# A hybrid decoder trunk: residual sums turned unscaled, by halves; norm weights applied at the eviction into high and low parts, reciprocal roots applied to the outputs of the projections

## The chip, the cores and the metric

The kernel runs on one core of a Trainium2 chip. The metric is the device time in microseconds of one execution. Its engines are named as the profile names them: PE (TensorE), DVE (VectorE), ACT (ScalarE), POOL (GpSimd) and SP (SyncE, which here only issues DMAs).

## The reference, cut to what matters

Two layers over 256 tokens of width 1024. The change is about how the norm in front of a projection is computed; the mixers in between keep their arithmetic.

```python
def rms_norm(x, g):
    y = x * lax.rsqrt(jnp.mean(x * x, axis=-1, keepdims=True) + NORM_EPS)
    return y * g

for l in range(DEPTH):                       # DEPTH = 2
    h = rms_norm(h_res, norm_mix[l])         # "norm 0" (l = 0), "norm 2" (l = 1)
    u = h @ w_in[l]                          # 1024 x 2536
    y = ...                                  # four mixers (MLA, NSA, RG-LRU, SSD) on columns of u
    h_res = h_res + y @ w_out[l]
    h = rms_norm(h_res, norm_ffn[l])         # "norm 1" (l = 0), the expert norm (l = 1)
    if l % 2 == 0:
        f = swiglu(h, ffn_w_gate[l // 2], ffn_w_up[l // 2], ffn_w_down[l // 2])
    else:
        f = moe_ffn(h, ...)                  # top 2 of 8 experts
    h_res = h_res + f
return rms_norm(h_res, norm_final)
```

The root of a row (a token) and the weight of a column commute with the product: `(x * r[t] * g[c]) @ W = r[t] * ((x * g[c]) @ W)`. The change uses this.

## The kernel before, in words

Tokens lie on the 128 partitions in two blocks (`tb` 0 and 1; `TB` = 2), each with 1024 columns in `xres`. All weights pass in pieces of 1 MB through a ring of seven slots (`ring`), loaded by SP in the order of use; a slot is loaded again once the DVE has read it (`lo_ready`). Products are made in three parts of reduced-precision float: ACT copies a piece into its high part (`w_hi`, `split`, L1228 and L1250), DVE subtracts to get the low part (`w_lo`, L1636 and L1661), and PE adds up high by high, high by low and low by high (`products3`, L413 to L415). One piece is 24 matmuls of 512 columns. Piece `p` of the mixer and its successors are called by their number here; `p + 1` is the second half of the inner dimension of the first columns.

Every engine runs its own written-out program in order and waits on semaphores. So what sets the order around the change is the place of a call in each engine's program.

**A norm before the change** (`turn_normed`, L386, on PE; `normed`, L1599, on DVE; `split_input`, L1230 and on, on ACT):

1. DVE adds the projection's sums to `xres` (`add_sums`, L1639 and on; L1643). The last piece is ordered so that block 0 is complete first and signals `proj_done`; block 1 is complete with the piece (`units_used`).
2. ACT squares and sums a block (`mean_square`, L1215); POOL turns the mean into the reciprocal root `rstd` (`roots`, L1122 and L1123).
3. DVE scales the block into `hn` (L1603; for norm 0 ACT does it, L1293).
4. PE turns `hn`, 16 transposes of 128 x 128 (L393), into four banks of PSUM.
5. DVE multiplies each bank by the norm weight into `hT` (L1612), ACT copies it into `hT_hi` (L1234), DVE subtracts into `hT_lo` (L1617). PE waits on `hT_lo_ready` for each half of the inner dimension before its products.

Banks 0 to 3 are those that DVE empties (`bank(0)`, `dve_took`), banks 4 to 7 those that ACT empties (`bank(1)`, `act_took`). The mixer's first projection (`by_token`) writes banks 4 to 7. The dense FFN (`ffn`) writes banks 0 to 3 first, and PE therefore waits in front of it until every bank that was given to DVE has been taken:

```python
                pe.wait_ge(act_took, gave[1])
                pe.wait_ge(dve_took, gave[0])
                if l == 0:
                    ffn(TB, BASE_FFN[0], hT_hi, hT_lo, BASE_FFN[0], 0)
```

At the start, SP loads `x`, then twelve small sets of parameter rows (`rows`, L1024, and `pe_row`, L1038), and only then the weights. PE turns the parameter rows into `par` (L404, L406; DVE L1589, L1590), which holds the norm weights among others.

In the mixer, ACT evicts the first projections into `utok` (L1314) and four banks into `xraw` (L1337); DVE evicts four banks into `lraw` (L1769), two into `xraw` (L1823) and two into `zs` (L1826). The convolutions read `lraw` and `xraw` (`conv`, L1798 and L1801). `cin` (L1832) needs ACT's `kvcT` (L1352).

In front of the experts the sums are already turned unscaled (L849), multiplied with the router (L862), and the root is applied to the logits.

## Time and profile before

| | us |
|---|---|
| median of 3 runs | 1603.23 (1601.26 to 1603.72) |
| the profiled execution, its own time | 1601.23 |
| its span in the trace | 1599.7 |
| DVE busy | 1249.2 (78%) |
| ACT busy | 1001.2 (63%) |
| POOL busy | 73.2 (5%) |
| mean granted TensorE clock | 0.971 of full speed |

A span begins with the first instruction and ends with the last; the execution's own time is 1.5 us longer. "Idle before" is the time that an engine stood still in front of an instruction, and behind the arrow stands the instruction that ended it.

### The profile page before, as it was taken

What the parts mean: (1) busy time and instruction counts of PE and PEld (TensorE: products, weight loads), DVE (VectorE), ACT (ScalarE), POOL (GpSimd) and SP (SyncE); (2) the same over time, 40 slices, a digit from 0 to 9 for tenths busy, and PEclk for the clock granted to TensorE, in tenths of its full rate; (3) what the DMA queues carried; (4) which work ended last, traced back from release to release, by engine and by line L of the source; (5) the groups of instructions that cost most, each with busy time, mean ns of one, the idle gap of its engine ahead of it and who ended that gap; (6) DMA issues with size and microseconds to landing.
All of it is one profiled execution on the core that took longest, in us unless ns stands there. A gap on an engine that the chain in (4) does not pass through costs nothing.

```text
span 1599.7 us, 20439 instructions
## 1 busy us (share of the span) xinstructions
PE 1538.3 (96%) x7566; PEld 1289.0 (81%) x7566; DVE 1249.2 (78%) x1286; ACT 1001.2 (63%) x911; POOL 73.2 (5%) x105
## 2 busy tenths in 40 slices
PE   7989899999899899999999999999999999999996
PEld 5978688888688787887888888888888888888884
DVE  6776744444458787999988988988988988989985
ACT  6456443344353556777777777778778777777763
POOL 2101000000000001000000000000000000000000
PEclk9987999999999799999999999999999999999998
DMA  9700655555452035999999999999999999999990
GB/s 294 242 1 15 187 190 194 191 184 183 131 168 70 1 101 186 393 397 348 393 396 347 394 397 346 394 397 345 394 398 344 395 397 344 396 396 345 395 389 29
DMA packets 189741, 444.25 MB, mean 278 GB/s; under 512 B 9617, under 2 KB 15902, under 8 KB 189678
## 3 DMA queue, kind: packets, MB, share of 16 engines
q1 hardware_dynamic: 185214, 427.82, 72.8%
q0 software_dynamic: 4464, 15.58, 3.8%
q8 instruction: 40, 0.66, 0.2%
q14 instruction: 23, 0.19, 0.0%
HBM read 435.51 MB, written 7.86 MB: 277 GB/s over the span
## 4 chain that ended last, share of the span: by engine, by line
PE 92%; DVE 5%; ACT 1%; issue 1%; SPq 0%; POOL 0%; DMA 0%; POOLq 0%; ACTq 0%; DVEq 0%
PE bank L414 26%; PE bank L415 26%; PE bank L413 26%; PE bank L543 2%; PE bank L470 2%; PE bank L546 1%; PE bank L682 1%; PE bank L664 1%; PE bank L641 1%; DVE work L1801 1%; PE bank L692 1%; PE bank L656 1%; DVE hT L1612 0%; PE bank L700 0%; DVE work L1854 0%
## 5 line engine op out<-in xcount | busy, mean ns | idle before, releaser
L1661 DVE TENSOR_TENSOR w_lo<-ring,w_hi 128x2048 fp32r<-128x2048 f32 x372 | 846.3, 2290 | 182.1 <-ACT w_hi L1250 180.9
L1250 ACT ACTIVATE w_hi<-ring 128x2048 fp32r<-128x2048 f32 x372 | 711.8, 1916 | 230.1 <-PE bank L413 230.1
L414 PE MATMUL bank<-w_hi,xT_hi 128*128 128x512 f32 x896 | 353.5, 394 | 0.5 <-DVE xT_lo L2225 0.5
L415 PE MATMUL bank<-w_hi,xT_lo 128*128 128x512 f32 x896 | 349.5, 390 | 0.0
L413 PE MATMUL bank<-w_lo,xT_hi 128*128 128x512 f32 x896 | 239.9, 389 | 0.0
L414 PE MATMUL bank<-w_hi,hidT_hi 128*128 128x512 f32 x560 | 220.8, 394 | 2.7 <-DVE hidT_lo L1668 2.7
L415 PE MATMUL bank<-w_hi,hidT_lo 128*128 128x512 f32 x560 | 218.4, 390 | 0.0
L413 PEld LDWEIGHTS bank<-w_lo,xT_hi 128*128 128x128 f32 x896 | 168.2, 188 | 35.5
L414 PEld LDWEIGHTS bank<-w_hi,xT_hi 128*128 128x128 f32 x896 | 168.2, 188 | 34.5 <-DVE xT_lo L2225 0.7
L415 PEld LDWEIGHTS bank<-w_hi,xT_lo 128*128 128x128 f32 x896 | 168.4, 188 | 33.8
L414 PE MATMUL bank<-w_hi,hT_hi 128*128 128x512 f32 (+2 forms) x384 | 149.5, 393 | 9.9 <-DVE hT_lo L1617 9.9
L415 PE MATMUL bank<-w_hi,hT_lo 128*128 128x512 f32 (+2 forms) x384 | 147.9, 388 | 0.0
L413 PE MATMUL bank<-w_lo,hidT_hi 128*128 128x512 f32 x560 | 147.8, 389 | 0.0
L414 PEld LDWEIGHTS bank<-w_hi,hidT_hi 128*128 128x128 f32 x560 | 105.2, 188 | 24.6 <-DVE hidT_lo L1668 3.4
L413 PEld LDWEIGHTS bank<-w_lo,hidT_hi 128*128 128x128 f32 x560 | 105.1, 188 | 22.3
L415 PEld LDWEIGHTS bank<-w_hi,hidT_lo 128*128 128x128 f32 x560 | 105.2, 188 | 21.3
L1256 ACT ACTIVATE hidT_hi<-bank 128x512 fp32r<-128x512 f32 x70 | 41.2, 599 | 101.4 <-PE bank L470 101.4
L1636 DVE TENSOR_TENSOR w_lo<-ring,w_hi 128x2048 fp32r<-128x2048 f32 (+1 forms) x34 | 77.1, 2280 | 30.2 <-ACT w_hi L1228 30.0
L414 PEld LDWEIGHTS bank<-w_hi,hT_hi 128*128 128x128 f32 x384 | 74.4, 194 | 24.8 <-issue 7.4
L413 PE MATMUL bank<-w_lo,hT_hi 128*128 128x512 f32 (+2 forms) x384 | 91.6, 380 | 0.0
L1228 ACT ACTIVATE w_hi<-ring 128x2048 fp32r<-128x2048 f32 (+1 forms) x34 | 64.4, 1900 | 39.7 <-PE bank L413 24.5
L415 PEld LDWEIGHTS bank<-w_hi,hT_lo 128*128 128x128 f32 x384 | 74.4, 194 | 13.9
(355 smaller groups left out, 1372.1 us busy)
## 6 DMA issues: line engine op xcount, KB each, us to landing
ring<-in_moe_w_gate_dram SPq DMA_DIRECT2D x112, 1024.0 KB, 9.5
ring<-in_moe_w_up_dram SPq DMA_DIRECT2D x112, 1024.0 KB, 9.4
ring<-in_moe_w_down_dram SPq DMA_DIRECT2D x112, 1024.0 KB, 9.1
ring<-in_ffn_w_gate_dram SPq DMA_DIRECT2D x14, 1024.0 KB, 5.1
ring<-in_ffn_w_up_dram SPq DMA_DIRECT2D x14, 1024.0 KB, 5.2
ring<-in_ffn_w_down_dram SPq DMA_DIRECT2D x14, 1024.0 KB, 4.9
ring<-in_w_in_dram SPq DMA_DIRECT2D x12, 1024.0 KB, 5.2
ring<-in_w_out_dram SPq DMA_DIRECT2D x8, 1024.0 KB, 8.4
```

The costliest lines, as they stand in the source:

```text
L413: return pe.matmul(o, x_hi, w, start=False, stop=stop)
L414: pe.matmul(o, x_hi, w, start=start, stop=False)
L415: return pe.matmul(o, x_lo, w, start=False, stop=False)
L470: mm = pe.transpose(banks[2 + v][:, f * P:(f + 1) * P], hid[:, v, f * P:(f + 1) * P], ident[:, :])
L543: mm = pe.matmul(b[i][:, 0:S], wk, hT_hi[:, 4 * h + k, :], start=start and not low, stop=stop and low)
L546: pe.matmul(b[i][:, 0:S], wk, hT_lo[:, 4 * h + k, :], start=False, stop=False)
L641: mm = pe.matmul(b[:, i * nk:(i + 1) * nk], q, k, start=True, stop=True)
L1228: act.activation(dst[:, :, 0:n], slot_k(p)[:, :, 0:n], ACT.Copy).then_inc(hi_ready, 1)
L1250: act.activation(w_hi[:, (base + at) % SPLIT, :], ring[:, i, :], ACT.Copy).then_inc(hi_ready, 1)
L1256: act.activation(hidT_hi[:, v, :], banks[2 + v][:, :], ACT.Copy).then_inc(hidT_hi_ready, 1)
L1636: dve.tensor_tensor(dst[:, :, 0:n], slot_k(p)[:, :, 0:n], hi[:, :, 0:n], ALU.subtract)\
L1661: dve.tensor_tensor(w_lo[:, v, :], ring[:, (base + at) % RING, :], w_hi[:, v, :].bitcast(F32), ALU.subtract).then_inc(lo_ready, 1)
```

## The change

Norms 0, 1 and 2 lose the scaling pass. PE turns `xres` itself, each half of a block as soon as its sum is added (`turn_sums`); ACT evicts each bank straight into `hT_hi` with the norm weight as scale, and DVE makes `hT_lo` from the same bank in one instruction (two instructions of 256 columns for a bank on either engine). The root now goes elsewhere: into the scale of the `utok` evictions, into SiLU's scale and the product behind it in the dense FFN, and, where the outputs have channels on the partitions, as a row `rrow` that PE spreads over the partitions from two diagonal matrices (`rdiag`). The last piece of each output projection is ordered by halves of a block, and `add_sums` waits for each half. DVE splits the first piece of the second mixer ahead of the sums. At the start, the parameter rows are issued from ACT's queue instead of SP's, `ident` is made first, and PE turns six blocks of `x` before the parameter rows.

```diff
+            def turn_half(norm, b, tb, g):
+                for k in range(2):
+                    mm = pe.transpose(b[:, (2 * k + tb) * P:(2 * k + tb + 1) * P],
+                                      xres[:, tb, (2 * g + k) * P:(2 * g + k + 1) * P], ident[:, :])
+                if tb == TB - 1:
+                    give(mm, 0)
+
+            def turn_sums(norm):
+                mark["raw", norm] = gave[0]
                 b = [bank(0) for _ in range(4)]
                 for tb in range(TB):
-                    pe.wait_ge(hn_ready, TB * norm + tb + 1)
...
+                    for h in range(2):
+                        pe.wait_ge(half_added, 4 * (norm - 1) + 2 * tb + h + 1)
+                        for g in (2 * h, 2 * h + 1):
+                            turn_half(norm, b[g], tb, g)
+            pe.wait_ge(ident_ready, 1)
+            pe.wait_ge(x_in, 16 * TB)
...
-                        if first:
-                            pe.wait_ge(hT_lo_ready, 8 * l + 2 * h + 2)
...
+                                    if first and tb == 0 and k % 2 == 0 and not low:
+                                        pe.wait_ge(dve_took, mark["raw", 2 * l] + 2 * h + k // 2 + 1)
...
+                pe.wait_ge(rdiag_ready, l + 1)
+                b = bank(1)
+                for tb in range(TB):
+                    mm = pe.matmul(b[:, tb * P:(tb + 1) * P], ones[:, :], rdiag[:, tb, :], start=True, stop=True)
+                give(mm, 1)
...
-            sp.wait_ge(prow_zero, 1)
-            rows("mix", norm_mix.rearrange("l (a b) -> a l b", b=P), 8)
...
+            act.wait_ge(prow_zero, 1)
+            rows("mix", norm_mix.rearrange("l (a b) -> a l b", b=P), 8)
...
-            def split_input(norm):
+            def split_turned(norm):
                 for g in range(4):
-                    act.wait_ge(dve_took, mark["turned", norm, g])
-                    act.activation(hT_hi[:, 2 * g:2 * g + 2, :], hT[:, 2 * g:2 * g + 2, :], ACT.Copy)\
-                        .then_inc(hT_hi_ready, 1)
+                    n = mark["raw", norm] + g
+                    act.wait_ge(*filled_by[0][n])
+                    for k in range(2):
+                        hi = act.activation(hT_hi[:, 2 * g + k, :], banks[n % 4][:, k * S:(k + 1) * S], ACT.Copy,
+                                            scale=par[:, l, c0 + 2 * g + k:c0 + 2 * g + k + 1])
+                    hi.then_inc(hT_hi_ready, 1)
...
+                b = filled()
+                act.activation(rrow[:, :], b[:, 0:S], ACT.Copy).then_inc(act_took, 1)
...
-            def normed(l2, turn_set):
-
-                for tb in range(TB if l2 else 0):
-                    dve.wait_ge(rstd_ready, 7 * (l2 // 2) + 5 * (l2 % 2) + tb + 1)
-                    signal(dve.tensor_scalar(hn[:, tb, :], xres[:, tb, :],
...
+            def split_turned(norm):
+                for g in range(4):
+                    b = filled()
+                    dve.wait_ge(hT_hi_ready, 4 * norm + g + 1)
+                    for k in range(2):
+                        at = 2 * g + k
+                        lo = dve.scalar_tensor_tensor(out=hT_lo[:, at, :], in0=b[:, k * S:(k + 1) * S],
+                                                      scalar=par[:, l, c0 + at:c0 + at + 1],
+                                                      in1=hT_hi[:, at, :].bitcast(F32), op0=ALU.mult, op1=ALU.subtract)
+                    take_bank(lo)
...
+            def add_sums(stage, unit):
+                for tb in range(TB):
+                    for half in range(2):
+                        if (tb, half) == (TB - 1, 1):
+                            dve.wait_ge(units_used, unit + 1)
+                        else:
+                            dve.wait_ge(proj_done, 3 * stage + 2 * tb + half + 1)
+                        r = xres[:, tb, half * 512:(half + 1) * 512]
+                        signal(dve.tensor_tensor(r, r, banks[4 + 2 * tb + half][:, :], ALU.add), "half", half_added)
...
-                    take_bank(dve.tensor_copy(lraw[:, i, 3:3 + S], b[:, 0:S]))
+                    take_bank(dve.tensor_tensor(lraw[:, i, 3:3 + S], b[:, 0:S], rrow[:, :], ALU.mult))
...
+                link(dve.tensor_tensor(xraw[:, 0:4, 3:3 + S], xraw[:, 0:4, 3:3 + S],
+                                       rrow.unsqueeze(1).broadcast_to([P, 4, S]), ALU.mult))
```

How the order of the instructions moves, at three places. A row is one instruction or several alike (`x8`), with its line, operation, what it writes and reads, and the size.

ACT, from the start of its program to the third piece of weights, before:

```order
L1215 ACT_TABLE_LOAD
L1215 ACTIVATE hn,stat<-xres 128x1024 x2
L1293 ACTIVATE hn<-xres,rstd 128x1024 x2
L1228 ACTIVATE w_hi<-ring 128x2048
L1234 ACTIVATE hT_hi<-hT 128x512 x4
L1228 ACTIVATE w_hi<-ring 128x2048
L1228 ACTIVATE w_hi<-ring 128x4x496
```

And now, from the last three of the twelve DMAs on:

```order
L1224 DMA prow<-in_mla_kv_norm_dram 1x256
L1224 DMA prow<-in_mla_q_norm_dram 2x2x96
L1238 DMA pe_row<-in_nsa_cmp_pe_dram 32x4x64
L1218 ACT_TABLE_LOAD
L1218 ACTIVATE hn,stat<-xres 128x1024 x2
L1250 ACTIVATE w_hi<-ring 128x2048
L1260 ACTIVATE hT_hi<-bank,par 128x256 x8
L1250 ACTIVATE w_hi<-ring 128x2048
L1250 ACTIVATE w_hi<-ring 128x4x496
```

The scaling L1293 is gone, the twelve DMA issues stand in front of the table load, and the first piece still stands ahead of the eviction into `hT_hi`.

ACT at norm 2 (between the dense FFN and the second mixer), before:

```order
L1256 ACTIVATE hidT_hi<-bank 128x512 x2
L1250 ACTIVATE w_hi<-ring 128x2048
L1228 ACTIVATE w_hi<-ring 128x2048
L1215 ACTIVATE hn,stat<-xres 128x1024 x2
L1228 ACTIVATE w_hi<-ring 128x2048
L1234 ACTIVATE hT_hi<-hT 128x512 x4
L1228 ACTIVATE w_hi<-ring 128x4x496 x2
```

And now:

```order
L1283 ACTIVATE hidT_hi<-bank 128x512 x2
L1277 ACTIVATE w_hi<-ring 128x2048
L1250 ACTIVATE w_hi<-ring 128x2048 x2
L1260 ACTIVATE hT_hi<-bank,par 128x256 x8
L1218 ACTIVATE hn,stat<-xres 128x1024 x2
L1250 ACTIVATE w_hi<-ring 128x4x496 x2
```

The squares moved from ahead of the turned sums to behind them, and both pieces of the first projection stand ahead.

DVE at the same place, before:

```order
L1643 TENSOR_TENSOR xres<-xres,bank 128x512 x4
L1705 MEMSET work 128x2x3
L1706 MEMSET work 128x6x3
L1636 TENSOR_TENSOR w_lo<-ring,w_hi 128x2048
L1710 MEMSET router 128x56
L1713 TENSOR_TENSOR router<-router,par 128x64
L1603 TENSOR_SCALAR hn<-xres,rstd 128x1024 x2
L1612 TENSOR_TENSOR hT<-bank,par 128x512 x3
L1617 TENSOR_TENSOR hT_lo<-hT,hT_hi 128x512
L1612 TENSOR_TENSOR hT<-bank,par 128x512
L1617 TENSOR_TENSOR hT_lo<-hT,hT_hi 128x512 x3
```

And now:

```order
L1677 TENSOR_TENSOR xres<-xres,bank 128x512 x2
L1678 COPY flag<-ones 128x1
L1677 TENSOR_TENSOR xres<-xres,bank 128x512 x2
L1678 COPY flag<-ones 128x1
L1644 SCALAR_TENSOR_TENSOR hT_lo<-bank,par,hT_hi 128x256 x8
L1665 TENSOR_TENSOR w_lo<-ring,w_hi 128x2048
L1743 MEMSET work 128x2x3
L1744 MEMSET work 128x6x3
L1665 TENSOR_TENSOR w_lo<-ring,w_hi 128x4x496
L1751 TENSOR_SCALAR hn<-ident,rstd 128x128 x2
```

Eight instructions of 256 columns stand where ten of 512 or 1024 did, and the split of a piece and the router's rows no longer lie between the sums and the norm.

## Rows read from the trace of the kernel before

**Rows 1.** The page: busy us of the engines, and the chain that ended last by engine.

```profile
PE 1538.3 (96%) x7566; PEld 1289.0 (81%) x7566; DVE 1249.2 (78%) x1286; ACT 1001.2 (63%) x911; POOL 73.2 (5%) x105
...
PE 92%; DVE 5%; ACT 1%; issue 1%; SPq 0%; POOL 0%; DMA 0%; POOLq 0%; ACTq 0%; DVEq 0%
```

**Rows 2.** Timeline of the start: start us, us, engine, line, operation, idle before.

```profile
1.70 0.37 SPq L1024 DMA_DIRECT2D prow<-in_norm_mix_dram  x1
...
5.30 0.32 SPq L1038 DMA_DIRECT2D pe_row<-in_nsa_cmp_pe_dram  x1
5.66 19.48 SPq L982 DMA_DIRECT2D ring<-in_w_in_dram  x10
...
8.09 0.66 PE L404 MATMUL bank<-ident,prow 128*128 128x128 f32 x2 [8.09 <-DMA pe_row<-in_nsa_cmp_pe_dram]
...
10.84 1.91 ACT L1228 ACTIVATE w_hi<-ring 128x2048 fp32r<-128x2048 f32 x1 [0.34 <-DMA ring<-in_w_in_dram]
...
16.63 0.79 PE L414 MATMUL bank<-w_hi,hT_hi 128*128 128x512 f32 x1 [3.08 <-DVE hT_lo L1617]
...
21.35 0.40 PE L415 MATMUL bank<-w_hi,hT_lo 128*128 128x512 f32 x1
...
26.54 2.23 DVE L1636 TENSOR_TENSOR w_lo<-ring,w_hi 128x1984 fp32r<-128x1984 f32 x1
...
29.74 3.65 ACT L1228 ACTIVATE w_hi<-ring 128x1984 fp32r<-128x1984 f32 x2
```

**Rows 3.** Timeline of PE and DVE at norm 1, before the dense FFN.

```profile
181.42 1.07 PE L413 MATMUL bank<-w_lo,hT_hi 128*128 128x512 f32 x4
...
182.60 1.41 DVE L1643 TENSOR_TENSOR xres<-xres,bank 128x512 f32<-128x512 f32 x2 [1.38 <-PE bank L413]
...
192.32 0.77 PE L414 MATMUL bank<-w_hi,hT_hi 128*128 128x512 f32 x1 [3.52 <-DVE hT_lo L1617]
...
196.29 0.39 PE L415 MATMUL bank<-w_hi,hT_lo 128*128 128x512 f32 x1
```

**Rows 4.** Timeline of PE and DVE at norm 2, before the second mixer.

```profile
429.48 1.07 PE L413 MATMUL bank<-w_lo,hidT_hi 128*128 128x512 f32 x4
...
432.38 2.29 DVE L1636 TENSOR_TENSOR w_lo<-ring,w_hi 128x2048 fp32r<-128x2048 f32 x1
...
442.86 0.76 PE L414 MATMUL bank<-w_hi,hT_hi 128*128 128x512 f32 x1 [3.28 <-DVE hT_lo L1617]
...
448.22 0.39 PE L415 MATMUL bank<-w_hi,hT_lo 128*128 128x512 f32 x1
```

**Rows 5.** Windows: engines' busy us (instructions), PEclk, DMA share, GB/s.

```profile
183.00:186.00 3.00, 1.06 (x6) 1.09 (x7) 1.72 (x3) 1.96 (x3) 1.02 (x3) 0.84 0.00 0
...
434.00:438.00 4.00, 2.07 (x10) 2.10 (x11) 2.47 (x5) 1.05 (x1) 1.74 (x2) 0.52 0.51 146
```

**Rows 6.** Durations of like instructions, from the timeline.

```profile
74.27 0.39 ACT L1344 ACTIVATE work<-bank 128x256 f32<-128x256 f32 x1 [0.37 <-PE bank L578]
74.55 0.38 ACT L1345 ACTIVATE work<-bank 128x256 f32<-128x256 f32 x1
74.64 1.53 DVE L1801 SCALAR_TENSOR_TENSOR work<-work,par 128x256 f32<-128x256 f32 x3
...
98.52 0.42 DVE L1877 TENSOR_TENSOR work<-bank,work 128x256 f32<-128x256 f32 x1
...
416.77 1.03 PE L470 MATMUL bank<-ident,work 128*128 128x128 f32 x8
```

**Rows 7.** Timeline of DVE in the mixers: the last evictions, and `cin` behind them.

```profile
78.64 0.90 DVE L1823 COPY work<-bank 128x256 f32<-128x256 f32 x2 [0.19 <-PE bank L543]
...
82.43 1.16 DVE L1832 TENSOR_TENSOR work<-work,pe_t 128x240 f32<-128x240 f32 x2 [1.93 <-ACT work L1355]
...
508.85 1.17 DVE L1832 TENSOR_TENSOR work<-work,pe_t 128x240 f32<-128x240 f32 x2 [1.93 <-ACT work L1355]
```

**Rows 8.** Timeline in front of the experts.

```profile
606.10 1.41 DVE L1643 TENSOR_TENSOR xres<-xres,bank 128x512 f32<-128x512 f32 x2 [1.57 <-PE bank L413]
```

More of the change, by code:

```diff
@@ L439, in project @@
                                 t = slice(i * P, (i + 1) * P)
+                                if n == TB and bank0 == 0 and c == 0 and i == 0 and k % 2 == 0 and not low:
+                                    pe.wait_ge(dve_took, mark["raw", 1] + 2 * h + k // 2 + 1)
                                 mm = products3(banks[bank0 + (c * n + i) % 2][:, :], x_hi[:, 4 * h + k, t],
@@ L460, in down @@
                                                c == 0 and h == 0 and f == 0, last and f == 1, low)
-                        if last and low and i < n - 1:
+                        if n == TB and last and low and (i, halves) != (n - 1, (1,)):
                             mm.then_inc(proj_done, 1)
@@ L810, in project_output @@
                     last = i == 3
-                    order = [(tb, low) for tb in range(TB) for low in (False, True)] if last else \
-                        [(tb, low) for low in (False, True) for tb in range(TB)]
-                    for tb, low in order:
+                    order = [(tb, low, (half,)) for tb in range(TB) for half in range(2) for low in (False, True)] \
+                        if last else [(tb, low, (0, 1)) for low in (False, True) for tb in range(TB)]
+                    for tb, low, halves in order:
                         w = parts_of(p, p, i, low).rearrange("p (k n) -> p k n", k=2)
-                        for half in range(2):
+                        for half in halves:
                             for k in range(2):
@@ L820, in project_output @@
                                                last and k == 1, low)
-                        if last and low and tb == 0:
+                        if last and low and (tb, halves) != (TB - 1, (1,)):
                             mm.then_inc(proj_done, 1)
```

215 lines of the change are left out of this document (106 added, 109 removed).

## The prediction, before the changed kernel ran

> **What bounds the kernel.** I read the page first: PE is busy for 96% of the span, and the chain that ended last lies on PE for 92% of it and on DVE for 5% [rows 1]. So PE's work is what the span consists of, and a change that leaves PE's matmuls as they are can gain only where PE stands still or runs slowly. I then read the timeline of PE and found three such places that belong to a norm. At each, PE ends one projection, waits for adding, squaring, root, scaling, turning, weighting and splitting, and starts the next: at the start (first product at 16.63) [rows 2]; at norm 1, from 182.49 (181.42 + 1.07) to 192.32, 9.8 us [rows 3]; at norm 2, from 430.55 to 442.86, 12.3 us [rows 4]. The windows add that the granted clock falls while PE idles (0.84 in 183 to 186, 0.52 in 434 to 438, so it is at the lower of its two levels, 1.2 GHz instead of 2.4) [rows 5]. The timeline of PE shows what this costs behind each gap: products at 2.4 GHz start 0.23 us apart (four in 1.07, the last of them 0.39 [rows 3]), at 1.2 GHz 0.43 us. Behind the start there are 11 intervals in 4.72 us (16.63 to 21.35), which would take 2.5 at the higher level: 2.2 us lost. Behind norm 1, 11 intervals in 3.97 (192.32 to 196.29): 1.4 lost. Behind norm 2, 13 intervals in 5.36 (442.86 to 448.22): 2.4 lost [rows 2 to 4].
>
> **Norm 2, step by step.** Call the end of the last matmul E (430.55). The new adds of the first three quarters lie inside the last piece: a half takes 6 of its 24 matmuls, 1.36 us, and an add 0.70 (1.41 for two, [rows 3]). The last one starts with the same delay as now (0.11 us, 182.49 to 182.60) and ends at E + 0.8. The 16 transposes cost 0.13 each at full clock [rows 6]; 12 of them wait for nothing and take until E + 1.5, the last four end near E + 2.0, but the first bank is complete after ten, at E + 1.3. ACT then evicts a bank with two instructions of 0.38 that start 0.28 apart [rows 6]: 0.66 for the first bank, E + 2.0. DVE follows with two of 256 columns. The nearest row is the same operation at this size in SBUF, 1.53 for three, so 1.0 for a bank with its wait [rows 6]: E + 3.0. The first product needs only this bank, and the next bank comes 1.0 us later, as long as four products take. So PE starts at E + 3.0 instead of E + 12.3: 9.3 saved. The split of the first piece, 2.29 on DVE between the adds and the norm [rows 4], costs nothing now, since it stands ahead of the adds where DVE waits. PE idles only from E + 2.0 to E + 3.0, less than in any of the gaps above behind which it was slow, so I give back the 2.4 of the slow products too. Sum for norm 2: -11.7. Squares and roots stay on ACT and POOL behind the evictions (E + 3.8 to about E + 7), hidden by the first two pieces, 10.9 us of PE, before anything reads a root.
>
> **Norm 1** has the same chain, but one more wait: the dense FFN writes banks 0 to 3, and PE first waits until DVE has taken all four. DVE gives the last one free at E + 3.0 + 3 x 1.0 = E + 6.0, and if its pairs overlap (0.85) at E + 5.5; I take 5.7. Saved: 9.8 - 5.7 = 4.1. PE idles for 3.7 us in front of it. The clock was still high in most of 183 to 186 [rows 5], and fell in an idle stretch of like length, so the loss lies between 0 and 2.4; I take 1.2, against 1.4 now. Sum: -4.3.
>
> **The start.** SP now issues the first weights where the first parameter row stood, at 1.70 instead of 5.66, and the first piece lands 5.2 us or less after its issue (5.66 to 10.84) [rows 2]. It has `x` (1 MB) in front of it, so it lands between 6.9 and 10.8; I take 8.7. The parameter rows take ACT twelve issues of 0.3 (1.2 to 4.9) as they took SP, and the table load moves behind them, which costs ACT's squares 0.4 us. They landed by 8.09 after the last issue at 5.30 [rows 2]; now I expect some 8.3. PE has turned six blocks of `x` by then, turns the parameters (1 us), and the other ten blocks by 11.7. ACT splits the first piece until 10.6 (1.91), evicts the first bank until 11.3, DVE its low part until 12.3. First product at 12.3 instead of 16.63: -4.3, with 11.5 and 16.6 as its bounds. The slow products behind it stay: in 1.9 of loss (the mean of the three) for 2.2: -0.3. Sum: -4.6. DVE's chain of small work (angles, lambda) ended at 26.54, and ACT's small work behind it at 29.74 [rows 2], where it takes the fourth piece. Now DVE does four banks (to 15.3), two splits (4.6) and 4.6 us of small work: 24.5. ACT takes the fourth piece at 27.7 and has it at 29.6, and PE wants it at 12.3 + 10.9 + 1.9 + 5.3 = 30.4. That is the thinnest cover of the change; gone, it would cost what is missing at this one place.
>
> **In front of the experts** the adds of block 1 run one after the other behind the piece (606.10 + 1.41) [rows 8]. Now one lies inside the piece, and the router's products start 0.7 earlier: -0.6.
>
> **What is added.** PE: two matmuls of 128 columns for each layer. No row shows them; transposes of that size cost 0.13 [rows 6], and products with a plain operand may cost two to three times that. Bounds 0.3 and 0.9 a layer, I take 0.4: +0.8. ACT: one eviction of 0.4 for each layer behind the last `utok`, beside PE's channel projections: 0. DVE: `lraw`, `xraw` and `zs` are multiplied where they were copied. A product from PSUM of 256 columns takes 0.42 [rows 6], a copy 0.45 [rows 7]: 0. The scaling of four `xraw` channels, 1024 columns, is new; 512 columns cost 0.70 and 2048 cost 2.29, so about 1.2. It delays the evictions behind it, but DVE then stands idle 1.93 us for ACT in both layers [rows 7]: 0, and if that cover were gone 1.2 a layer. The 14 products with SiLU's output in the FFN get a scalar and keep their size, beside PE: 0.
>
> For the eviction in two pieces the rows say 0.66 on ACT and 1.0 on DVE for a bank, as against 0.70 for one instruction of 512. The Trainium skill speaks against such pieces (VectorE: DVE Perf Modes, "The TRN2 errata"): many small tiles pay the fixed latency each time, and it advises at least 512 elements. By its formula for two-source fp32, (N + 151) / 0.96, a pair would cost 0.85 us, and norm 1 would gain 0.4 us more than by the rows; the formula is for a plain two-tensor operation, and no run here shows it for this one.
>
> **Sum.** -11.7 - 4.3 - 4.6 - 0.6 + 0.8 = -20.4. Against the profiled execution's own 1601.2 this is 1580.8; the median of the runs is 2.0 above that execution, so I forecast 1582.5 for a median.
>
> **Rivals.**
> 1. *The parameter rows come late.* Now megabytes of weights are in flight beside them, while before they were ahead of every weight. If they land 4 us later, the first product stays at 16.6, and the result is 1587. For it: the queue is full from the start. Against it: they are small. The Trainium skill says (DMA: Bandwidth & Descriptors, "Issuing engines are not separate DMA queues") that transfers issued by different engines run on the same 16 engines and interleave; by that they would be slowed and not held up.
> 2. *The same on the other side.* If they are served only behind the ring's pieces, whose ten issues end at 25.14 (5.66 + 19.48) and the last of which lands 5.2 later, they land at about 33 (25.1 + 5.2 + 2.7, as now from issue to use), and the first product comes 3.5 later, at 36.5: 19.9 late. The other terms give 15.8 back: +4.1, 1607. From a first product at 32.4 on (16.6 + 15.8) the kernel is slower than before. No row shows a transfer held up like this.
> 3. *The mixers take it back.* DVE's chain there is tight: it came to the last evictions 0.19 us before PE had filled the bank [rows 7]. If products from PSUM cost 0.3 more than copies (8 of them) and the 1.2 of the scaling is not hidden, this is +3.6 a layer: 1590.
> 4. *The clock stays low.* If PE falls to 1.2 GHz at norm 1 and norm 2 as before, 2.4 and 1.2 come back: 1586.
>
> **Chances.** The forecast (1577 to 1585) 0.6; rival 1 0.12, rival 3 0.12, rival 4 0.1; rival 2 and anything else that ends above 1606.4, 0.03; within 0.2% (3.2 us, about what a measurement of this kernel can tell from no change) 0.03. Faster is all the rest, 0.94. The range must take in rivals 1, 3 and 4, and below the forecast a start at 11.5, banks freed at E + 5.3 and no slow products at norm 1: 1575 to 1590.
>
> **What would show it.** The first product near 12.3; the gap at norm 2 of about 3 us with products 0.23 apart behind it, and of 5.7 at norm 1; `cin` with 0.7 us of idle time left in front of it; the parameter rows' transposes before 9. A first product after 16, a gap at norm 2 above 5, or a second layer's mixer that is longer than before would make it wrong.

## The result, and the profile after

The changed kernel took 1587.28 us (median of 4 runs, 1584.44 to 1589.42) beside 1603.34 for the kernel before: a ratio of 0.9903, 95% interval 0.9888 to 0.9919. The forecast was 1582.5 with a range from 1575 to 1590: faster, as forecast, but by 16.1 us, not by 20.8. Twelve more runs in two later groups had medians of 1589.09 and 1589.57, so the median of all 16 is 1589.1 and the shortfall rather 6.6 than 4.8.

| | before | after |
|---|---|---|
| profiled execution, own time / span (us) | 1601.23 / 1599.7 | 1585.41 / 1583.6 |
| mean granted clock | 0.971 | 0.974 |
| first product | 16.63 | 15.97 |
| gap at norm 1 | 9.83 | 5.80 |
| gap at norm 2 | 12.31 | 3.12 |

The page of after, against [rows 1]: busy us of PE, and the chain by engine. PE has 8 more matmul records and 1.7 us less busy time; the share of the span is 97%.

```profile
PE 1536.6 (97%) x7574; PEld 1290.4 (81%) x7574; DVE 1246.5 (79%) x1292; ACT 1002.8 (63%) x923; POOL 74.3 (5%) x105
...
PE 93%; DVE 4%; ACT 1%; issue 1%; DMA 0%; ACTq 0%; POOL 0%; POOLq 0%; DVEq 0%
```

The timeline of the start (start us, us, engine, line, operation, idle before), against [rows 2]:

```profile
5.33 0.33 ACTq L1238 DMA_DIRECT2D pe_row<-in_nsa_cmp_pe_dram  x1
...
10.07 1.91 ACT L1250 ACTIVATE w_hi<-ring 128x2048 fp32r<-128x2048 f32 x1 [0.75 <-DMA ring<-in_w_in_dram]
...
12.20 0.66 PE L417 MATMUL bank<-ident,prow 128*128 128x128 f32 x2 [4.57 <-DMA pe_row<-in_nsa_cmp_pe_dram]
...
13.96 3.02 ACT L1260 ACTIVATE hT_hi<-bank,par 128x256 fp32r<-128x256 f32 x8 [1.99 <-DVE pe_t L1626]
...
15.97 0.77 PE L432 MATMUL bank<-w_hi,hT_hi 128*128 128x512 f32 x1 [0.44 <-DVE hT_lo L1644]
```

The last parameter row is issued at 5.33, as before, but PE can turn the rows only at 12.20, not at 8.09. The first piece is ready to be split at 10.07, so it is the rows that hold the start. Behind the first sixteen products PE also waits a little for the low part of the first piece, which it did not before:

```profile
20.94 2.12 PE L431 MATMUL bank<-w_lo,hT_hi 128*128 128x512 f32 x8 [0.38 <-DVE w_lo L1665]
```

The timeline at norm 1, against [rows 3]:

```profile
180.19 1.91 PE L391 MATMUL bank<-ident,xres 128*128 128x128 f32 x16
180.46 0.69 DVE L1677 TENSOR_TENSOR xres<-xres,bank 128x512 f32<-128x512 f32 x1 [0.69 <-PE bank L431]
...
181.48 3.02 ACT L1260 ACTIVATE hT_hi<-bank,par 128x256 fp32r<-128x256 f32 x8 [4.57 <-PE bank L391]
182.44 3.61 DVE L1644 SCALAR_TENSOR_TENSOR hT_lo<-bank,par,hT_hi 128x256 fp32r<-128x256 f32 x8 [1.12 <-ACT hT_hi L1260]
...
186.15 0.76 PE L432 MATMUL bank<-w_hi,hT_hi 128*128 128x512 f32 x1 [4.06 <-DVE hT_lo L1644]
```

The projection ends at E = 180.35 (the row of its last two products, 179.72 + 0.63). Only one add lies behind it. ACT's eight instructions take 3.02 and DVE's eight 3.61, a bank each 0.9 us; PE waits for the last of them, 4.06, and its first product is slow (0.76).

The timeline at norm 2, against [rows 4]:

```profile
424.90 0.62 PE L431 MATMUL bank<-w_lo,hidT_hi 128*128 128x512 f32 x2
...
427.62 2.70 DVE L1644 SCALAR_TENSOR_TENSOR hT_lo<-bank,par,hT_hi 128x256 fp32r<-128x256 f32 x6 [1.11 <-ACT hT_hi L1260]
...
428.64 0.47 PE L432 MATMUL bank<-w_hi,hT_hi 128*128 128x512 f32 x1 [1.38 <-DVE hT_lo L1644]
428.95 0.39 PE L433 MATMUL bank<-w_hi,hT_lo 128*128 128x512 f32 x1
```

E = 425.52, first product E + 3.12, and the next ones 0.23 apart at once. In the mixers DVE's idle time in front of `cin` (`work`, L1877) is 0.8 where it was 1.93 [rows 7]:

```profile
DVE work L1877 <- ACT work L1390: 1.5, 2, 0.8
```

(total, times, longest: the waits of DVE.)

**Where the time went.** I cut the span of each trace at points that all kernels share: the first product of the third piece (the first with 496 columns), the ends E of the last products in front of each norm, the first product behind it, and in the second layer the first product with `strict`, the mask of the experts' routing. Beside after's first trace stand those of the same kernel in a second and a third group of runs, at 1589.07 and 1588.70, close to the median of all. The last column splits the recorded sum of -20.4 over the same stages.

| stage (us) | before | after | after, again | after, third | after less before | forecast |
|---|---|---|---|---|---|---|
| to the third piece | 29.75 | 28.34 | 28.14 | 28.33 | -1.4, -1.6, -1.4 | -4.6 |
| mixer 0 to its E | 152.74 | 152.01 | 152.63 | 155.06 | -0.7, -0.1, +2.3 | +0.4 |
| gap at norm 1 | 9.83 | 5.80 | 5.81 | 5.81 | -4.0, -4.0, -4.0 | -4.1 |
| dense FFN to E | 238.23 | 239.37 | 238.35 | 239.67 | +1.1, +0.1, +1.4 | -0.2 |
| gap at norm 2 | 12.31 | 3.12 | 3.12 | 3.12 | -9.2, -9.2, -9.2 | -9.3 |
| mixer 1 to routing | 171.24 | 170.92 | 173.97 | 171.63 | -0.3, +2.7, +0.4 | -2.6 |
| the rest | 985.6 | 984.0 | 985.3 | 983.3 | -1.6, -0.3, -2.3 | 0 |

The two gaps are right within 0.1. Two things are not in any trace: the start, 3.0 to 3.2 short, and the second mixer, 2.3 to 5.3 short. The dense FFN is 0.3 to 1.6 short, and the first mixer in the third trace 1.9. Both mixers differ by about 3 us between executions of the same program. The windows show why, for the second one. They are, from the first product of the second mixer, the first 5 us, then 80 to 120 and 120 to 145 (columns: PE busy us and instructions, PEclk, DMA share, GB/s). Before:

```profile
442.90:447.90 5.00, 5.00 (x12) 0.51 0.17 16
522.90:562.90 40.00, 33.74 (x265) 0.79 0.01 2
562.90:587.90 25.00, 24.13 (x143) 0.86 0.13 42
```

After:

```profile
428.60:433.60 5.00, 4.96 (x22) 1.00 0.01 3
508.60:548.60 40.00, 36.13 (x247) 0.70 0.01 1
548.60:573.60 25.00, 24.13 (x148) 0.86 0.12 36
```

After, again:

```profile
428.10:433.10 5.00, 5.00 (x22) 1.00 0.01 3
508.10:548.10 40.00, 37.02 (x220) 0.62 0.00 1
548.10:573.10 25.00, 24.17 (x162) 0.80 0.00 1
```

At 0.5 the clock is at its lower level, so (1 - PEclk) x 2 x length is the time spent there: 4.9 + 16.8 + 7.0 = 28.7 us before; 24.0 + 7.0 = 31.0 after; 30.4 + 10.0 = 40.4 in the other execution. The stretches lie in and behind the attention stage, where PE first idles and is then busy at the lower clock. In before the 5 us behind norm 2 are part of the sum: without them its mixer has 23.8 us at the lower clock, and the changed kernel's 31 to 40 (34 in the third trace). The third trace's long first mixer has 41 us at the lower clock, the other two have 34. There is one trace of the kernel before, and its runs vary too, so its 23.8 is one sample.

### The profile page after: what moved, and what is told of

It is laid out like the page before. It is cut to its first block, busy times and chain, and to the rows that moved or that the text cites. A ratio compares the mean times of both kernels' runs of the same rounds, so it can differ in the third digit from the quotient of the medians.

```text
span 1583.6 us, 20483 instructions
## 1 busy us (share of the span) xinstructions
PE 1536.6 (97%) x7574; PEld 1290.4 (81%) x7574; DVE 1246.5 (79%) x1292; ACT 1002.8 (63%) x923; POOL 74.3 (5%) x105
## 4 chain that ended last, share of the span: by engine, by line
PE 93%; DVE 4%; ACT 1%; issue 1%; DMA 0%; ACTq 0%; POOL 0%; POOLq 0%; DVEq 0%
PE bank L432 26%; PE bank L433 26%; PE bank L431 26%; PE bank L562 2%; PE bank L488 2%; PE bank L707 1%; PE bank L565 1%; PE bank L666 1%; PE bank L689 1%; PE bank L681 1%; DVE work L1843 1%; PE bank L717 1%; PE bank L725 0%; DVE work L1899 0%; DVE hT_lo L1644 0%
## 5 line engine op out<-in xcount | busy, mean ns | idle before, releaser
L433 PEld LDWEIGHTS bank<-w_hi,hT_lo 128*128 128x128 f32 x384 | 73.5, 191 | 13.5
```

The source lines that it names most:

```text
L433: return pe.matmul(o, x_lo, w, start=False, stop=False)
```

## The experiments

Two theories. **A:** each stage's gain is what its trace shows; what is missing is (1) the late parameter rows, (2) the bank wait and the clock at norm 1, (3) low clock in the attention stages, which varies from run to run and takes back part of what norm 2 gains. **B:** the spread and the shortfall are something general (DMA load, noise), so local edits do not move the stages named.

### The parameter rows

`e1_weights_wait`: nothing of the weights is in flight beside the rows.

```diff
+            sp.wait_ge(prow_in, 16 * N_PROW)
             mixer_loads(0)
```

> The changed kernel, but SP issues the first weights only when all parameter rows have landed; the rows still go through ACT's queue. Theory A (the rows are late because they share the DMA engines with the weights): they land within 3 us of the last issue again, so PE turns them near 8.3 instead of 12.2; the weights are then issued near 8.2, land at 13.4, and the first product comes near 17. Theory B (ACT's queue itself is slow for these rows): PE turns them near 12 as in the changed kernel, the weights land at 17, the first product comes near 20.

A single run: 1592.35. Timeline of its start:

```profile
8.04 0.66 PE L417 MATMUL bank<-ident,prow 128*128 128x128 f32 x2 [0.56 <-DMA pe_row<-in_nsa_cmp_pe_dram]
...
12.96 1.91 ACT L1251 ACTIVATE w_hi<-ring 128x2048 fp32r<-128x2048 f32 x1 [3.90 <-DMA ring<-in_w_in_dram]
...
16.77 0.77 PE L432 MATMUL bank<-w_hi,hT_hi 128*128 128x512 f32 x1 [5.39 <-DVE hT_lo L1645]
```

The last row is issued at 5.08 by ACT's queue and used 2.96 later. With the ring's loads in flight it was used 6.87 after its issue (5.33 to 12.20). So the weights beside them are the cause, as theory A has it. The Trainium skill (DMA: Bandwidth & Descriptors, "Issuing engines are not separate DMA queues") says that DMAs issued by different engines run on the same 16 DMA engines and interleave. The traces agree as far as that goes: the rows were slowed by some 4 us, not held up behind megabytes.

`e2_rows_sp`: SP issues the rows itself, in front of the weights (ACT issues none).

```diff
-            act.dma_start(prow[r0:r0 + n, :, 0:cols], src).then_inc(prow_in, 16)
+            sp.dma_start(prow[r0:r0 + n, :, 0:cols], src).then_inc(prow_in, 16)
...
+            rows("mix", norm_mix.rearrange("l (a b) -> a l b", b=P), 8)
...
             mixer_loads(0)
```

> The changed kernel with the parameter rows issued by SP ahead of the weights, as in the kernel before. By theory A the rows land by 8.1, the first piece of weights at 10.8, ACT has split it at 12.8, evicted the first bank at 13.7, DVE its low part at 14.6: first product at 14.6 instead of 15.97, some 1.4 us faster than the changed kernel (about 1586). If the rows were not what held the start, the first product stays at 16 or comes later, since the weights are issued 4 us later: 1587 to 1590.

```profile
14.60 0.77 PE L432 MATMUL bank<-w_hi,hT_hi 128*128 128x512 f32 x1 [3.74 <-DVE hT_lo L1644]
```

Median 1589.11 (1582.24 to 1590.73, 6 runs), ratio to before 0.9906 (0.9889 to 0.9922). The first product came at 14.60, as expected, but PE had idled 3.74 in front of it; 12 intervals between the products behind it were slow, and the third piece started at 28.05, only 0.1 to 0.3 before the changed kernel's. In the changed kernel PE turns ten blocks right before its first product and only 3 to 8 intervals are slow. So a start that is 0.9 to 1.4 earlier at the first product is worth 0.1 to 0.3. The time did not follow the expectation of about 1586 either.

`e7_start`: the same, with eight filler products (identity times a constant, into a bank not in use yet) behind the last transpose.

> SP issues the parameter rows in front of the first weights, and eight filler products keep PE busy between the transposes and the first product. Theory A: the rows are there at 7.5 us, the first product comes at about 14.6 and the slow products behind it go (about 12 of 0.43 us become 4 or none): the third piece starts at 25.5 to 26.5 where the changed kernel has 28.3. Rival: DVE's low part of the weights (20.8 us) holds the second dozen of products, and the third piece starts no earlier than 27.5. The whole time follows by 1 to 2.5 us, if the mixers' clock allows it to be seen.

```profile
8.97 2.40 PE L391 MATMUL bank<-ident,xres 128*128 128x128 f32 x10
11.16 4.91 PE L428 MATMUL bank<-cbias,ident 128*128 128x256 f32 x16
15.72 0.58 PE L434 MATMUL bank<-w_hi,hT_hi 128*128 128x512 f32 x1
16.14 0.39 PE L435 MATMUL bank<-w_hi,hT_lo 128*128 128x512 f32 x1
```

I had sized the fillers wrongly: one of 256 columns stands as two records (16 for eight) and lasts 0.47 at the high clock, not 0.23, so they ran 1.1 beyond the point of need. Even so the slow products went and the third piece started at 27.01, between both expectations. Median 1588.86 (1584.30 to 1597.78, 8 runs), ratio 0.9924 (0.9901 to 0.9948): a gain of 1.1 in a stage drowns in a spread of 13.5 us.

### Norm 1

`e3_no_bank_wait`: PE no longer waits for all four banks; the FFN's own waits for each bank, which are there already, order its writes.

```diff
                 pe.wait_ge(act_took, gave[1])
-                pe.wait_ge(dve_took, gave[0])
+                if l > 0:
+                    pe.wait_ge(dve_took, gave[0])
```

> The changed kernel without the wait of PE, ahead of the dense FFN, for all four banks; each bank is still waited for by the product that first needs it. Theory: the wait is what makes the gap at norm 1 5.8 us against 3.1 at norm 2, and the longer gap is what lets the clock fall. Then the gap becomes 3.1, products behind it start 0.23 apart, and the kernel is 2.7 + 2.4 = 5.1 us faster than the changed one (1582). Rival: the clock falls whatever the gap is, because of the whole pattern at norm 1: then only 2.7 (1584.5). If DVE's low parts pace the products anyway, less than 2.

```profile
182.79 1.91 PE L391 MATMUL bank<-ident,xres 128*128 128x128 f32 x16
186.07 0.47 PE L432 MATMUL bank<-w_hi,hT_hi 128*128 128x512 f32 x1 [1.38 <-DVE hT_lo L1645]
186.38 0.40 PE L433 MATMUL bank<-w_hi,hT_lo 128*128 128x512 f32 x1
```

The gap is 3.12 (E 182.95) and no product is slow; the FFN takes 236.89, where the changed kernel took 239.37, 238.35 and 239.67. In the two stages together -4.1 to -5.5, as expected. Yet the median is 1586.96 (1579.63 to 1592.82, 6 runs; ratio 0.9890, 0.9864 to 0.9916). The profiled run, at 1588.21, shows what took it: mixer 0 lasted 155.21, 3.2, 2.6 and 0.2 more than in the three traces of after, and mixer 1 176.88, 6.0, 2.9 and 5.3 more. Here, from 80 us on, its mixer 1:

```profile
506.10:546.10 40.00, 36.98 (x217) 0.62 0.00 1
546.10:571.10 25.00, 24.17 (x150) 0.66 0.00 1
```

That is 30.4 + 17.0 = 47.4 us at the lower clock. Two of the six runs, at a mean clock of 0.978, took 1579.6; no trace shows one of them. Whether the edit makes the mixers' low stretches longer, or this run met long ones, is open.

`e4_fill`: sixteen fillers behind the transposes of norm 1 instead.

> The changed kernel with 16 matmuls of 256 columns into a bank that nothing reads, put into the idle time at norm 1 (3.7 us of work in a gap of 4.1), and the wait for the banks kept. It separates the clock from the wait: if the clock falls because PE stands idle, the products behind norm 1 now start 0.23 apart and the kernel is 2.4 us faster (1585) with the gap unchanged at 5.8. If the fall has another cause, there is no gain, and up to 0.3 is lost.

```profile
181.11 1.91 PE L391 MATMUL bank<-ident,xres 128*128 128x128 f32 x16
182.85 7.07 PE L861 MATMUL bank<-cbias,ident 128*128 128x256 f32 x32
189.58 0.58 PE L432 MATMUL bank<-w_hi,hT_hi 128*128 128x512 f32 x1
```

Mis-sized in the same way: 7.07 us of filler made the gap 8.31 instead of 5.81. The clock stayed up, and the FFN took 236.98. This measures the clock's part by itself: 1.4 to 2.7 us. Median 1593.28 (1584.52 to 1597.31, 6 runs; ratio 0.9939, 0.9918 to 0.9960). By its two stages this kernel should equal the changed one; the median is some 4 over it, in runs with a mean clock down to 0.967. The trace is of the fastest run, so where the others lost it is not shown.

### The halves

`e5_whole_sums`: PE turns only when all four half blocks are added.

```diff
                 b = [bank(0) for _ in range(4)]
+                pe.wait_ge(half_added, 4 * (norm - 1) + 4)
```

> PE turns the sums at norms 1 and 2 only when all four half blocks are added; nothing else is changed. Theory A (the halves hide three quarters of the transposes): 12 of the 16 transposes come behind the last sum, so the gap at norm 2 grows from 3.1 us by 1.0 to 1.4, the one at norm 1 from 5.8 by as much, and PE stays idle long enough that the first products of norm 2 start at the low clock, another 1 to 2.4: 3 to 5 us over the changed kernel. Rival: DVE's subtraction into the low parts, not the transposes, sets the pace behind the last sum, and the halves bring under 0.5 at each norm.

```profile
427.03 0.61 PE L432 MATMUL bank<-w_lo,hidT_hi 128*128 128x512 f32 x2
428.69 1.94 PE L391 MATMUL bank<-ident,xres 128*128 128x128 f32 x16 [1.05 <-DVE xres L1678]
432.01 0.47 PE L433 MATMUL bank<-w_hi,hT_hi 128*128 128x512 f32 x1 [1.37 <-DVE hT_lo L1645]
```

Gaps of 7.08 and 4.37: +1.27 and +1.25, the expected size, so what the transposes hide is worth 1.3 at each norm. The clock did not fall at norm 2 (0.47), so that part of the expectation failed. Median 1593.87 (1584.27 to 1595.65, 6 runs; ratio 0.9938, 0.9914 to 0.9963), 4.8 over the changed kernel on the same chip (1589.09), of which the gaps are 2.5; the rest is not placed.

### The clock in the mixers

The changed kernel twice more, as the reference of a group each:

> The changed kernel itself, so that the three beside it are compared on the same chip. All theories: a median near 1587. Theory A (what a run takes is set by the stages read from the trace, and on top of it by whether the second low stretch of TensorE's clock in each mixer is short or long): the runs fall into groups about 5 to 6 us apart, with mean granted clocks of about 0.970 and 0.974. Theory B (the spread is noise of no one place): times spread evenly.

> The changed kernel once more, as the reference for the three beside it on the same chip: a median between 1587 and 1590.

1589.09 (1588.09 to 1590.12, 6 runs, ratio 0.9918, 0.9902 to 0.9934) and 1589.57 (1582.97 to 1591.40, 6 runs, ratio 0.9911, 0.9892 to 0.9930). Of all 16 runs, 13 have a mean clock of 0.970 or 0.971 and 1588.1 to 1591.4 us; three have 0.974 to 0.976 and 1583.0 to 1585.4. So two groups 5 us apart, as theory A says; but their median is 2 above its 1587. The kernel before has its own: of 35 runs 24 lie between 0.965 and 0.969, at about 1604, and eight at 0.971, at 1601.0. At 0.971 the changed kernel took 1589.1 (mean of 8), 11.9 less.

The traces put sizes to it. Mixer 1 lasted 170.92, 171.63, 173.97 and 176.87 us (after, after third, after again, `e2_rows_sp`), with 31, 34, 41 and 48 us at the lower clock (summed from first product to routing in windows of 1 us): from 34 to 41 it cost 2.3 and from 41 to 48 another 2.9. The first and the last of them start their mixer at the same time, 428.64. The two window rows of `e2_rows_sp` read as those of `e3_no_bank_wait`, 0.62 and 0.66.

The Trainium skill (TensorE: Matmul & The Clock Gate, Part 1, "What's actually happening") says that the number of slow matmuls at a kernel's start differs from run to run of one kernel, and puts the penalty of that ramp under 1% of a typical kernel. The traces agree as to the start: 3, 8 and 4 slow intervals behind the first product in three executions of one program. The spread seen here is larger, 17 us or 1.1% between two runs of one kernel (`f1_best`, below), whose mean clocks are 0.976 and 0.965, and where traces exist it lies in the mixers and not at the start.

`e8_late_start`: PE waits at norm 2 for the roots, as long as it must, and so idles there again.

```diff
                 if l > 0:
                     turn_sums(2 * l)
+                    pe.wait_ge(rstd_ready, 7 * l + 2)
```

> PE waits at norm 2 for both reciprocal roots, which are there about 8.8 us after the end of the products (434.3 in the changed kernel's trace), before it starts the second mixer; nothing else is changed. Theory A (what the kernel before lost at the low clock behind its gap at norm 2 is in part given back in the mixer, since a clock that fell there falls less in the attention stage): the gap grows from 3.1 to about 9 us and some 12 slow products follow it, but the low clock in the rest of the mixer takes about 24 us as in the kernel before, not 31 to 48; so the whole is only 3 to 7 us slower than the changed kernel. Theory B (the low stretches in the attention stage do not depend on norm 2): gap and slow products in full, 8.3 us slower, and the rest of the mixer at 34 to 48 us of low clock as in the changed kernel.

```profile
429.39 1.91 PE L391 MATMUL bank<-ident,xres 128*128 128x128 f32 x16
438.37 0.79 PE L432 MATMUL bank<-w_hi,hT_hi 128*128 128x512 f32 x1 [7.07 <-POOL rstd L1127]
```

```profile
438.40:443.40 5.00, 5.00 (x16) 0.68 0.98 303
518.40:558.40 40.00, 36.21 (x219) 0.66 0.00 1
558.40:583.40 25.00, 22.92 (x182) 1.00 0.05 13
```

The gap is 8.82 (+5.70), and 8 intervals of the products behind it are slow (+1.6). (The roots come at E + 8.8, not at the E + 7 of the prediction; in the changed kernel nothing waits for them there.) The median is 1593.90 (1593.32 to 1596.56, 5 runs; ratio 0.9941, 0.9927 to 0.9956), 4.3 over the changed kernel on the same chip, not 7.3: by the medians 3 us came back. The two traces do not show so much: this one (1596.56, the slowest run of the five) is 7.9 over the changed kernel's of this group (1588.70), with 5.7 of it in the gap, 0.7 at the start and 1.9 behind the routing, and mixer 1 only 0.4 shorter, though 1.6 of slow products are in it. So 2.0 came back there. In its trace 27 us of the rest of the mixer are at the lower clock (expected 24), as against 34 in the changed kernel's trace of this group, and the third stretch is missing (PEclk 1.00 in the last window). Its mixer 1 took 171.24, what it took before the change. This points the way of theory A; but the stretches vary by themselves too, so that one trace for each side does not settle it.

`e6_mixers_filled`: fillers into PE's idle time in the attention stage, eight where it waits 2.0 us for the probabilities and five in front of the step sums.

> Thirteen more filler products per layer in PE's idle time inside the attention stage of each mixer (eight before the second product of probabilities, where PE waits 2.0 us, five before the step sums, where it waits 1 to 1.9 us); they write to a bank that the next product overwrites. Theory A (the clock falls because PE idled just before, and the low stretch that follows costs far more than the idle time): the low stretch at 101 to 133 us and at 510 to 542 us shrinks or goes, the runs gather at the fast end: 5 to 15 us under the changed kernel, mean granted clock 0.98 or more. Theory B (the low stretch belongs to this stage whatever PE does in the gaps): the clock as before, and the time the same or up to 3 us longer for the filler itself.

```profile
97.89 3.72 PE L689 MATMUL bank<-cbias,ident 128*128 128x256 f32 x16
...
106.19 3.81 PE L689 MATMUL bank<-cbias,ident 128*128 128x256 f32 x10 [1.97 <-DVE work L1902]
```

Median 1586.89 (1583.27 to 1589.46, 5 runs; ratio 0.9895, 0.9875 to 0.9914), clock 0.978 to 0.982, the highest of all. So the clock went as theory A has it, and the time did not: 2.2 under the changed kernel (1589.09) instead of 5 to 15. The fillers did not fit: the first lasts 3.72 for a wait of 2.0, and the second stands behind a wait for a bank (1.97 still idle) and adds 3.81 on top. In the profiled run, the slowest of the five, mixer 0 took 158.39 with 38 us at the lower clock, and mixer 1 171.41 with 24: a filler that is too long can cost more than the clock gives.

`f1_best`: the edits of `e2_rows_sp` and `e3_no_bank_wait`, two fillers behind the last transpose at the start, and ACT's first evictions ahead of its split:

```diff
                     act.wait_ge(dve_took, 1)
-                    split(p)
-                    split_turned(0)
+                    split_turned(0, (0, 1))
+                    split(p)
+                    split_turned(0, (2, 3))
```

> Three edits together: parameter rows issued by SP in front of the weights; ACT evicts the first two banks of x before it splits the first piece, with two filler products on PE while it waits; and PE does not wait for all four banks in front of the dense FFN. Theory A (gains read stage by stage add up): the first product at about 13.0 where the changed kernel has 15.5 to 16.0, the third piece at 26.3 to 27; the gap at norm 1 3.1 instead of 5.8 and no slow products behind it, together -5.1; the sum 6 to 7 us under the changed kernel at the same length of the low clock stretches in the mixers, a median of 1581 to 1584. Rival (as the four runs of the bank wait alone near 1588 suggest): the mixers' low stretches grow by one step of 3 us in most runs, and the median stays at 1585 or above.

`f2_best_busy`: the same, with four fillers a layer where PE waits 2.0.

```diff
                     if n == 0:
                         keep_busy(b, 10)
+                    if n == 1:
+                        keep_busy(b, 4)
                     pe.wait_ge(act_took, mark["probT", l, n])
```

> The kernel before it in this list, with four filler products per layer before the second product of probabilities, where PE waits 2.0 us (one of them takes 0.47 us at the high clock, so they take 1.9). Theory A (idle time in the attention stage makes the clock fall there): less low clock in each mixer, 2 to 6 us under the version without them. Rival: PE idles again 1 to 2 us in front of the step sums, the clock falls there instead, and the two versions agree within 1.5 us, or this one is slower by the filler that runs at the low clock.

| | first product | third piece | gap, norm 1 | FFN | mixer 0 | mixer 1 | median (lowest to highest) | clock |
|---|---|---|---|---|---|---|---|---|
| after (three traces) | 16.0, 15.5, 16.0 | 28.3, 28.1, 28.3 | 5.8 | 239.4, 238.4, 239.7 | 152.0, 152.6, 155.1 | 170.9, 174.0, 171.6 | 1589.57 (1582.97 to 1591.40) | 0.970 to 0.976 |
| f1 | 13.32 | 25.73 | 3.12 | 236.89 | 152.02 | 170.84 | 1586.84 (1575.95 to 1593.20) | 0.965 to 0.976 |
| f2 | 13.34 | 25.71 | 3.12 | 236.90 | 152.93 | 170.83 | 1578.04 (1577.67 to 1578.71) | 0.978 to 0.979 |

(Times and clocks of after in the last two columns are those of its third group, beside which f1 and f2 ran.) `f1_best` has every local gain: its profiled execution, 1575.95, is the fastest run of all. But its six runs spread over 17 us, and the median is 2.7 under the changed kernel instead of 6 to 7: the rival's number held. Each slower run has a lower or equal mean clock, down to 0.965; as only the fastest was profiled, the rival's longer stretches in the mixers are not shown. `f2_best_busy` has the same stages and four fillers a layer more. Its median is 8.8 under f1's, and all its five runs lie within 1.04 us. Ratio to before 0.9844 (0.9829 to 0.9859), f1's 0.9905 (0.9880 to 0.9931); its highest run is 4.3 us below the lowest of the changed kernel's 16. Here the place in `f1_best`:

```profile
93.50 1.99 PE L668 MATMUL bank<-work 64*128 64x256 f32 x8
97.50 3.65 PE L709 MATMUL bank<-work 128*128 128x64 f32 x16 [2.01 <-ACT work L1419]
```

and in `f2_best_busy`:

```profile
95.40 1.99 PE L691 MATMUL bank<-cbias,ident 128*128 128x256 f32 x8
97.40 2.00 PE L711 MATMUL bank<-work 128*128 128x64 f32 x16
...
103.81 0.56 PE L757 MATMUL bank<-work,upper 128*128 128x4 f32 x2 [2.44 <-DVE work L1905]
```

The fillers end as the wait does; the sixteen products behind them take 2.00 instead of 3.65. The clock falls later, in the idle 2.44 us (PEclk 1.00 from 99 to 101, 0.84 from 101 to 103, 0.50 behind). In its mixer 1 the trace has 27 us at the lower clock, in its mixer 0 31, where `f1_best` at its fastest had 34 in each.

The same place in the first mixer of the kernel before:

```profile
101.06 1.97 PE L682 MATMUL bank<-work 128*128 128x64 f32 x16 [2.00 <-ACT work L1380]
```

Here the clock stayed high behind the same idle 2.00 us. In the traces without fillers at this place these sixteen products took anything from 1.97 (before, `e2_rows_sp`, `e4_fill`) to 3.65, and the second mixer of one program took 2.75, 3.65 and 2.48; with fillers in front of them they took 1.89 or 2.00 in both mixers of both traces. So the idle time there lets the clock fall in some executions and not in others, and filling it takes this choice away. What that is worth is only shown in sum. At the place itself it is nothing: the step sums wait for DVE and start 6.3 us after the sixteen products in f1 (103.82) and 6.4 in f2 (103.81). f2's profiled run is also 2.1 slower than f1's fastest: mixer 0 is 0.9 longer and the time behind the routing 1.3. The fillers thus take away f1's long times, and nothing from its shortest. That idle time in the attention stage is what makes the runs of all these kernels differ is likely by this, and not shown: none of f1's longer executions was profiled, six runs of the changed kernel without fillers once lay within 2.0 us (`after_again`), and the same fillers without f1's other edits were not run.

Of the two theories, A holds for the stages: each local edit moved the stage that it names, by about the expected size. It does not hold for the medians, which follow the mixers' low stretches as well.

## Why the prediction was right, and where it was short

- **Norm 2 (-11.7): right in its place.** Gap 3.12 (forecast 3.0), products 0.23 apart from the first on. A bank took DVE 0.9 (1.0 assumed from the SBUF row). The formula of the Trainium skill (VectorE: DVE Perf Modes, "The TRN2 errata"), worked out for a pair in the prediction, gave an estimate of 0.85: the trace lies between it and the row. The term "I give back the 2.4 of the slow products too" is true behind the gap and failed for the whole: mixer 1 became 0.3 shorter in one trace and 2.7 and 0.4 longer in the others, not 2.4 shorter. I had treated the low clock as a loss of that one place. The attention stage behind it has low stretches of its own: 24 us in before's trace beyond its first 5 us, 31 to 48 us in the traces of kernels with the new norm 2 unfilled. That they exist could be seen in the windows of before, and I priced no change of them. Beyond before's 24 us the three traces of after have 7, 17 and 10 us more of low clock, and miss 2.3, 5.3 and 3.0 us of the forecast in this stage: about 0.3 us for each us. By the prediction's own list, "a second layer's mixer that is longer than before" would make it wrong, and two of three traces have one.
- **Norm 1 (-4.3): the gap right** (5.80 for 5.7, with 5.5 by the formula). The clock term, taken as 1.2 from bounds of 0 and 2.4, was 1.4 to 2.7 by `e3_no_bank_wait` and `e4_fill`: rival 4 held at this norm, not at the other.
- **The start (-4.6): wrong, rival 1.** "Now I expect some 8.3" for the rows was 12.06 by the chain of waits, and PE turned them at 12.20, not before 9. The first piece was ready at 10.07 (10.80 and 10.22 in the other traces), not at 8.7 (bounds 6.9 and 10.8): issued 4.0 earlier, it came at most 0.8 earlier. With the rows on time the first product would have come at about 13.7 (10.07 + 1.91 + 0.7 + 1.0), so the rows cost 2.3 of the 3.7 and the piece 1.4. `f1_best` reached 13.32. A fast start alone gains little, as `e2_rows_sp` shows, since the products behind it run at the low clock; the prediction had them stay slow, but not the wait for DVE's low part (0.38, and 0.4 to 0.9 in f1 and f2). Rival 1's own number, a first product at 16.6, was too late by 0.6, since the rows came 4.0 late as it supposed but ACT had its first piece split by then. Rival 2, rows behind the whole ring, did not happen.
- **Rival 3** did not happen: `cin` kept 0.8 of idle time (0.7 forecast), so the scaling of `xraw`, 1.22 in the trace for 1.2, was hidden and cost PE nothing. The cover for the fourth piece held.
- **The experts (-0.6) and the added products (+0.8): right.** From the end of the last products to the router's first, 2.44 before (605.62 to 608.06) became 1.70 (591.74 to 593.44). The two added products of the first layer hold PE for 0.36 (38.91 to 39.27), for 0.4 forecast.
- **Small slips in the sums.** The mean of the three losses behind the gaps is 2.0, not 1.9; 1580.8 and 2.0 are 1582.8, not 1582.5; and the three terms named for the lower end of the range add up to 2.4, so that they lead to 1580 and not to 1575. None of them moves the forecast by more than 0.3.
- **The sum:** -20.4 forecast against the profiled execution, -15.8 measured in the first one and -12.2 and -12.5 in the two near the median. By the stages of the table 3.0 to 3.2 are missing at the start, 0.3 to 1.6 in the FFN behind norm 1, 2.3 to 5.3 in mixer 1; the other stages together gave 0.2 to 2.5 more than forecast. The way and most of the size (the two gaps, -13.2 of the 16.1) were right by their mechanism. That the result lay within the range is in part luck: it held because rivals 1 and 4 were in it, while the variation in the mixers was in no rival and took up the same room; the median of all 16 runs is 0.9 from the upper end, and 1587, rival 1's own number, was met although only a third to a half of the missing time lies at the start.

## What to carry to other kernels

When an edit closes a gap in front of a stage that has idle time of its own, price the clock there too: list the stretches at the lower clock in every stage, and read a local gain from the trace's stages, not from medians that differ by one such stretch. Try to fill an idle wait of PE with just as much work as it lasts, ahead of the wait and not behind another one; here the kernel with the four fillers that fitted had a median 8.8 us lower and a spread of 1 us instead of 17, while in the kernel where one was nearly twice too long and one stood behind another wait the clock rose and the time fell by 2 only. A small load on which everything hangs should be issued ahead of bulk loads and not beside them; but look at what the earlier start meets next.

## What the runs showed of the hardware

- The last of twelve small row loads was used 6.9 us after its issue with 1 MB loads in flight, and 3.0 after it with none; it was slowed, not queued to the end.
- One program spent 31, 34 or 41 us of its second mixer at the lower clock in three executions, and 34, 34 or 41 of its first. Two kernels that start the second mixer at the same 428.64 spent 31 and 48 us of it there (`after`, `e2_rows_sp`), 5.95 us apart.
- PE idle for 1.4 us behind its transposes (norm 2, and norm 1 in `e3_no_bank_wait`) left the clock high; idle for 4.06 (norm 1) or 3.74 (`e2_rows_sp`) it was low behind; with fillers instead of the idle time it stayed high. Idle for 2.0 us in the attention stage it was low behind in some executions and high in others.
